# Cross output projection in token chunks, with part of the routing inside it, an earlier barrier, and SyncE's row stores ahead of two weight loads

## The chip, the cores and the metric

The kernel runs on one core of a Trainium2 chip. The metric is the device time of the whole program in microseconds. The program is one launch that runs both layers.

## The reference, cut to what matters

Two decoder layers run over 1024 prompt tokens and 32 sample tokens (1056 in all, model width 1024, float32). The end of each layer is this:

```python
x = x + cross_attn(rmsnorm(x, g_x), mem_k, mem_v, w_xq, w_xo)   # ends in o @ w_xo, 512 -> 1024
h = rmsnorm(x, g_ffn)
g_sel  = argmax(h @ w_rg + b_rg)                # 1 group of 4
e_logit = (h @ w_re + b_re) of the group g_sel  # 8 experts
top_p, top_i = top_k(softmax(e_logit), 2)       # 2 experts a token, gates from top_p
y = sum over both of gate * (silu(h @ w_eg[e]) * (h @ w_eu[e])) @ w_ed[e]
x = x + y
```

The 36 columns of w_rg and w_re together give the logits. 32 experts have 2 MB of gate and up weights and 1 MB of down weights each, so a layer reads 100 MB of them.

## The kernel before, in words

Every engine has its own program, and counters (semaphores) order them. Both layers run the same code.

**The projection.** `x` lies with the model width on the partitions: 8 blocks (`j`) by 1056 tokens. Blocks go one after the other. For each, TensorE computes three chunks of 352 tokens (`x_out`, L1392, 4 matmuls a chunk; a float32 matmul is two instructions in the trace) into one of two sets of three PSUM banks. VectorE adds all 1056 columns into `x` (L2522). ScalarE writes the block times its gain to `xn` (L1869) and its square to `xsq` (L1870). VectorE adds the squares to `xsum` (L2507, `add_xsq`). TensorE multiplies the router weights (36 columns, stationary) with `xn` (`logits`, L1403).

**Root and routing.** After the last block TensorE sums the squares by token (L1422), ScalarE takes the root (L1876), VectorE its reciprocal (L2530), and the logits are turned so that tokens lie on the partitions (L1427), nine tiles of 128 tokens, the last with 32. From L2533 to L2570 VectorE picks the group and the two experts of all nine tiles at once. TensorE counts picks by expert (L1445, L1447). VectorE ranks the experts by count (`place`, L2577 and L2578, 32 by 32 compares), works out a slot for each pick, and builds one-hot matrices that two TensorE matmul groups (L1457) turn into the table `idx` of token numbers (written at L2629).

**Rows to DRAM.** TensorE turns `xn` into token rows (`rows_of`, L1437), ScalarE scales them (L1886), and SyncE stores nine tiles to `xrow` (L684). Four row buffers are shared.

**The queue of SyncE**, in order: gate weights of experts 0 and 1 (L669, `load_gu`) after the first block; gate weights of experts 2 and 3 after the sums by token; nine row stores; down weights of experts 0 to 3 (L672, `load_dn`); when two gathers have landed (L689), gate weights of expert 4; when `routed` is set (L691), its down weights; then for each later expert, by popularity, a read of `order_i`, a wait for a free slot and its two loads. There are five slots. SyncE does nothing else while it waits, so everything behind a wait is held.

**The barrier.** When `idx` is ready, GpSimd starts the first two gathers of rows (L2874). VectorE goes on: the order of the experts (L2632 to L2635), the gates and the overflow list (L2637 to L2647, which sets `routed`), and only then `stage_end(dve, 9)`. All engines but SyncE wait there for each other. TensorE fills waits with idle matmuls (`keep_clock`, L777).

**The experts.** 22 blocks of 128 slots in each layer. For block n: TensorE turns the gathered rows (`turn_x`, L1470), VectorE copies them (`take_x`, L2654), TensorE does gate and up (L1484), ScalarE the exponential (L1896), VectorE `hidden` (L2660 to L2663), TensorE `turn_h` (L1494) and down (L1508), GpSimd scatters the result (L2880). Block n uses the experts of four groups: the first six experts have 3 or 4 groups each, the last nine 2 each. At the end of layer 0 SyncE also loads 5 MB for the next layer, whose first matmuls are L1547.

## Time and profile before

| what | value |
|---|---|
| median of 3 runs | 2490.47 us (2487.63 to 2491.78) |
| profiled execution, its own time | 2477.46 us |
| its span, first to last instruction | 2475.7 us |
| mean granted TensorE clock | 0.979 of full speed |
| TensorE busy | 2301.5 us, 93% |
| VectorE, ScalarE, GpSimd busy | 47%, 27%, 19% |
| stage of the change in layer 0 | about 824 to 940 us, experts to 1215 |
| same in layer 1 | about 2042 to 2157 us, experts to 2433 |

A timeline line is: start, duration, engine, line, operation, tiles, number of instructions, and in brackets the idle time before it and what ended it. A busy TensorE can be one that runs idle matmuls to keep its clock, so its share alone does not say what bounds a stage.

### The profile page before, as it was taken

The page shows a single profiled execution, that of the slowest core. Times are in us where ns is not written, and L with a number is a line of the kernel's source. Part 1 is how long each engine was busy: PE and PEld are TensorE (multiplying, and loading weights), DVE is VectorE, ACT ScalarE, POOL GpSimd, SP SyncE. Part 2 cuts the span into 40 slices and gives each one's busy share as a digit, 9 for nine tenths or more (in the row PEclk, how much of TensorE's full clock was granted, in tenths as well). Part 3 has the DMA queues.
Part 4 walks back from the last instruction along what each step waited for, and adds up shares of the span by engine and source line. Part 5 has one row for each costly group of instructions (what it writes and reads, how often), then busy time and mean ns, then how long its engine had stood idle before and what let it go on. Part 6 is the DMA issues. An engine that isn't in the chain of part 4 may idle for free.

```text
span 2475.7 us, 41476 instructions
## 1 busy us (share of the span) xinstructions
PE 2301.5 (93%) x17596; PEld 1359.3 (55%) x17596; DVE 1168.0 (47%) x2072; ACT 657.2 (27%) x1404; POOL 480.7 (19%) x590
## 2 busy tenths in 40 slices
PE   8999998889999999999899999988799999999984
PEld 5644565656666664333366456666566675733332
DVE  2455556874232354333263655568742342633334
ACT  1023554422012230111130335544220032211113
POOL 6003423520100001111260034235100000011113
PEclk9999999989999999999999999999899999999997
DMA  5001001163142148999840010011621411799996
GB/s 196 11 20 28 15 12 44 44 247 133 36 164 86 68 163 328 406 422 423 335 142 11 20 30 12 12 44 47 257 88 44 154 69 68 270 358 410 423 415 258
DMA packets 80288, 390.82 MB, mean 158 GB/s; under 512 B 20942, under 2 KB 25164, under 8 KB 60588
## 3 DMA queue, kind: packets, MB, share of 16 engines
q1 hardware_dynamic: 61948, 309.38, 32.5%
q0 software_dynamic: 17568, 76.57, 8.1%
q8 instruction: 143, 2.34, 0.4%
q10 hardware_dynamic: 576, 2.10, 0.2%
q14 instruction: 53, 0.43, 0.1%
HBM read 355.31 MB, written 41.41 MB: 160 GB/s over the span
## 4 chain that ended last, share of the span: by engine, by line
PE 76%; DVE 9%; issue 5%; ACT 3%; PEld 2%; DMA 2%; POOL 1%; POOLq 1%; PEldq 1%; SPq 0%; ACTq 0%; DVEq 0%
PE ps L1484 13%; PE ps L801 9%; PE ps L824 8%; PE ps L1508 6%; PE ps L1392 5%; PE ps L972 5%; PE ps L892 5%; PE ps L1192 3%; PE ps L984 2%; PE ps L950 2%; PE ps L1000 2%; PEld ps L824 2%; DVE arena L2225 2%; PE ps L1470 2%; PE ps L1214 1%
## 5 line engine op out<-in xcount | busy, mean ns | idle before, releaser
L1484 PE MATMUL ps<-arena 128*32 128x512 f32 x2304 | 316.9, 602 | 22.6 <-issue 16.8
L824 PE MATMUL ps<-arena,ring 128*128 128x352 f32 x936 | 277.9, 459 | 1.0 <-ACTq L489 1.0
L801 PE MATMUL ps<-x,ring 128*128 128x352 f32 x768 | 231.6, 463 | 11.1 <-DMA x<-in_x 9.6
L824 PEld LDWEIGHTS ps<-arena,ring 128*128 128x128 f32 x936 | 177.7, 190 | 99.4 <-ACTq L489 1.2
L2654 DVE COPY arena<-ps 128x1024 f32<-128x1024 f32 x44 | 53.9, 1224 | 336.9 <-PE ps L1470 336.9
L801 PEld LDWEIGHTS ps<-x,ring 128*128 128x128 f32 x768 | 146.9, 192 | 93.2 <-issue 13.3
L1484 PEld LDWEIGHTS ps<-arena 128*32 128x32 f32 x2304 | 92.4, 111 | 187.1 <-issue 187.1
L1508 PE MATMUL ps<-arena 128*32 128x512 f32 x1408 | 160.2, 595 | 3.8 <-ACT arena L1901 3.8
L2874 POOL DMA_INDIRECT arena<-xrow,arena x46 | 46.8, 1017 | 591.5 <-DVE arena L2629 319.9
L972 PE MATMUL ps<-arena 96*128 96x512 f32 (+3 forms) x384 | 144.9, 487 | 0.0
L1392 PE MATMUL ps<-arena,ring 128*128 128x352 f32 x384 | 117.7, 463 | 1.6 <-DVE arena L2487 1.6
L1484 PE MATMUL ps<-ring,arena 128*32 128x512 f32 x512 | 116.0, 607 | 0.0
L1670 ACT ACTIVATE ring<-ps 128x512 f32<-128x512 f32 (+2 forms) x192 | 87.7, 489 | 104.1 <-PE ps L984 104.1
L892 PE MATMUL ps<-arena,x 128*128 128x512 f32 x256 | 112.9, 601 | 2.2 <-ACT arena L1618 2.2
L1192 PE MATMUL ps<-arena 64*32 64x256 f32 x2560 | 90.2, 414 | 24.1 <-DVE arena L2359 15.1
L1675 ACT ACTIVATE ring<-ps,nmax 128x128 f32<-128x128 f32 (+7 forms) x128 | 94.7, 740 | 57.8 <-DVE nmax L2128 56.8
L2359 DVE STREAM_TRANSPOSE arena<-arena 128x1024 f32<-128x1024 f32 x80 | 95.9, 1227 | 24.4 <-PE ps L1192 23.1
L1896 ACT ACTIVATE arena<-ps 128x256 f32<-128x256 f32 x44 | 16.9, 383 | 329.1 <-PE ps L1484 329.1
L984 PE MATMUL ps<-consts,ring 128*128 128x128 f32 x576 | 89.7, 281 | 12.9 <-ACT ring L1670 6.5
L2127 DVE TENSOR_REDUCE nmax<-ps 128x1 f32<-128x128 f32 (+7 forms) x128 | 97.0, 758 | 4.4
L2126 DVE TENSOR_TENSOR ps<-ps,consts 128x128 f32<-128x128 f32 x128 | 38.2, 299 | 127.6 <-PE ps L972 126.5
L1392 PEld LDWEIGHTS ps<-arena,ring 128*128 128x128 f32 x384 | 71.7, 190 | 46.1 <-issue 6.8
(470 smaller groups left out, 3661.9 us busy)
## 6 DMA issues: line engine op xcount, KB each, us to landing
arena<-in_w_gu SPq DMA_DIRECT2D x52, 2048.0 KB, 14.3
arena<-in_w_dn SPq DMA_DIRECT2D x64, 1024.0 KB, 11.1
ring<-in_ring SPq DMA_DIRECT2D x56, 512.0 KB, 3.6
ring<-in_w_gu SPq DMA_DIRECT2D x12, 2048.0 KB, 13.9
arena<-yrow SPq DMA_DIRECT2D x16, 1024.0 KB, 9.3
arena<-in_mem_k SPq DMA_DIRECT2D x16, 512.0 KB, 7.2
arena<-in_mem_v SPq DMA_DIRECT2D x16, 512.0 KB, 9.2
xrow<-arena SPq DMA_DIRECT2D x16, 512.0 KB, 8.5
```

What stands on the lines that cost most here:

```text
L801: mm = pe.matmul(ps[:, PIECE_BANKS[n % len(PIECE_BANKS)], 0:CH], ring[:, j % RING, k, :], x[:, k, tok], start=k == 0, stop=k == KT - 1)
L824: mm = pe.matmul(ps[:, (j % 2) * NCH + c, 0:CH], ring[:, j // per, (j % per) * units + k, :], src[:, k, tok], start=k == k0, stop=k == uni ...
L892: mm = pe.matmul(ps[:, 6 + t % 2, :], x[:, k, t * P:t * P + m], wvg[:, k, :], start=k == 0, stop=k == KT - 1)
L972: mm = pe.matmul(ps[:, bank + at // 512, 0:end - at], q_h[0:QK, b, qb * P:(qb + 1) * P], k_h[0:QK, b, at:end], start=True, stop=True)
L984: mm = pe.transpose(ps[:, bank, (kb % 4) * P:(kb % 4 + 1) * P], prob[:, e, kb * P:(kb + 1) * P], ident)
L1192: mm = pe.matmul(ps[ND * g:ND * (g + 1), 4 + 2 * (n % 2) + h, 256 * x:256 * (x + 1)], q8[b][x][r, n, :], ct[r, m % NCT, 8 * g:8 * (g + 1), ...
L1392: mm = pe.matmul(ps[:, (j % 2) * NCH + c, 0:CH], ring[:, slot, (j % 2) * XH + k, :], co[:, k, tok], start=k == 0, stop=k == XH - 1)
L1484: mm = pe.matmul(ps[r, 2 + n % 2, :], xb_t[:, n % 2, k, r], w_gu[e % NW][:, k, :], start=k == 0, stop=k == KT - 1, skip_group_check=True)
L1508: mm = pe.matmul(ps[r, 4 + f, :], h_t[:, k, r], w_dn[e % NW][:, k, f * 512:(f + 1) * 512], start=k == 0, stop=k == 1, skip_group_check=True)
L1675: act.activation(prob[:, e, 0:w], ps[:, 2 * e:2 * e + 2, :].rearrange("p a n -> p (a n)")[:, 0:w], ACT.Exp, bias=nmax[:, e, 1:2], scale=ML ...
L2127: step(dve.reduce_max(nmax[:, e, 0:1], sc, AX))
L2359: dve.transpose(ct[:, m % NCT], keys).then_inc(ct_ready, 1)
```

## The change

The projection's loop is turned. Tokens are cut into tiles 0 to 2, 3 to 5 and 6 to 8 (384, 384 and 288 columns), and all eight blocks of one token chunk are done before the next: 24 units, three PSUM banks. Logits are computed with `xn` stationary and the router weights moving, so that they come out with tokens on the partitions. The turn of the logits and the copies before it go. After the fourth unit of the last chunk, root and routing of tiles 0 to 5 (`EARLY`) are done between the remaining units; tiles 6 to 8 follow after the last one. The counts and ranks are computed in two parts. `place` comes from a 32 by 32 compare with one column and a matmul. VectorE's barrier stands right after `idx`. The gates, the overflow list and `routed` move behind `hidden(0)`. In SyncE's queue the nine row stores come ahead of the gate weights of experts 2 and 3.

```diff
+XO_TILES = ((0, 3), (3, 6), (6, NT + 1))
+XO_UNITS = tuple((c, j) for c in range(len(XO_TILES)) for j in range(XO_MT))
+XO_BANKS = 3
+EARLY = XO_TILES[2][0]
...
-                sp.wait_ge(lin_done, IN_N + OUT_MT + XK_MT + XQ_MT + 1)
+                sp.wait_ge(xo_done, 1)
                 load_gu(0, 0)
                 load_gu(1, 1)
-                sp.wait_ge(ssq_ready, 2 * NCH + 1)
-                load_gu(2, 2)
-                load_gu(3, 3)
                 for t in range(NT + 1):
                     m = P if t < NT else ND
                     sp.wait_ge(xr_evac, t + 1)
                     sp.dma_start(xrow[t * P:t * P + m, :], xr[0:m, t % 4, :]).then_inc(row_moved[t % 4], 16)
+                load_gu(2, 2)
+                load_gu(3, 3)
                 for e in range(4):
                     load_dn(e, e)
...
+                def logits(u):
+                    c, k = XO_UNITS[u]
+                    pe.wait_ge(xg_ready, u + 1)
+                    for t in range(*XO_TILES[c]):
+                        m = P if t < NT else ND
+                        mm = pe.matmul(ps[0:m, 3 if t < EARLY else 4, t * NR:(t + 1) * NR], xn[:, k, t * P:t * P + m], w_r[:, k, :],
+                                       start=k == 0 and t in (0, EARLY), stop=k == KT - 1, skip_group_check=True)
...
+                for u in range(len(XO_UNITS)):
+                    x_out(u)
+                    if u == 0:
+                        x_back(NT)
+                    if u >= 1:
+                        logits(u - 1)
+                    if XO_UNITS[u] == (2, 2):
+                        pe.wait_ge(sq_added, NCH + 1 + 2)
+                        token_sums(0, EARLY)
+                keep_clock(3, 4)
+                pe.wait_ge(sq_added, NCH + 1 + 3)
+                token_sums(EARLY, NT + 1)
+                logits(len(XO_UNITS) - 1)
...
-                for t in range(6):
+                for t in range(5):
                     rows_of(t)
-                keep_clock(5, 9)
                 pe.wait_ge(part_or_counts_ready, len(PART) + 1)
+                count_tiles(0, EARLY, 0)
+                rows_of(5)
+                pe.wait_ge(part_or_counts_ready, len(PART) + 2)
+                count_tiles(EARLY, NT + 1, 1).then_inc(ranked, 1)
+                count_above(0, EARLY)
+                count_above(EARLY, NT + 1).then_inc(ranked, 1)
-                keep_clock(3, 12)
+                keep_clock(3, 3)
+                pe.wait_ge(beaten_or_hot_ready, 1)
+                pe.matmul(ps[:, 2, 0:NE], ones[0:NE, :], beaten[0:NE, :], start=True, stop=True).then_inc(ranked, 1)
...
-                keep_clock(3, 34)
+                keep_clock(3, 22)
                 stage_end(pe, 9)
...
+                for u in range(len(XO_UNITS)):
+                    add_out(u)
+                    if u >= 1:
+                        add_xsq(u - 1)
+                    if XO_UNITS[u] == (2, 3):
+                        dve.wait_ge(std_ready, 2 * NCH + 1)
+                        step(dve.reciprocal(rstd_t[:, 0:EARLY], rstd_t[:, 0:EARLY]))
+                        dve.sem_inc(norm_ready, 1)
+                        dve.wait_ge(lg_done, 1)
+                        take_logits(0, EARLY, 3)
+                    elif XO_UNITS[u] == (2, 4):
+                        pick_group(0, EARLY)
+                    elif XO_UNITS[u] == (2, 5):
+                        first_of_max(e_all, NE, 0, EARLY, m1, oh1)
+                    elif XO_UNITS[u] == (2, 6):
+                        pick_second(0, EARLY)
+                        step(count_picks(0, EARLY))
...
-                step(dve.tensor_tensor(beats, key.unsqueeze(1).broadcast_to([P, NE, NE]), key.unsqueeze(2).broadcast_to([P, NE, NE]), ALU.is_gt))
-                step(dve.tensor_reduce(place, beats, AX, ALU.add))
+                step(dve.tensor_tensor(key_own[0:NE, :], key[0:NE, :], ident[0:NE, 0:NE], ALU.mult))
+                step(dve.tensor_reduce(key_col[0:NE, :], key_own[0:NE, :], AX, ALU.add))
+                dve.tensor_scalar(beaten[0:NE, :], key[0:NE, :], key_col[0:NE, 0:1], None, ALU.is_lt).then_inc(beaten_or_hot_ready, 1)
+                dve.wait_ge(ranked, 3)
...
                 dve.tensor_copy(idx, table).then_inc(idx_ready, 1)
 
+                stage_end(dve, 9)
+
...
-                dve.tensor_copy(over_i[:, :], over_c).then_inc(routed, 1)
-                step.restart()
-                stage_end(dve, 9)
-
+
+                def weigh_and_spill():
+
+                    dve.wait_ge(rx_out, 1)
...
+                    dve.tensor_copy(over_i[:, :], over_c).then_inc(routed, 1)
...
                     hidden(n)
+                    if n == 0:
+                        weigh_and_spill()
```

## Rows read from the trace of the kernel before

**Rows 1.** The page's first line.

```profile
span 2475.7 us, 41476 instructions
```

**Rows 2.** Windows: stretch, length, five engines' busy time, clock, DMA share, GB/s.

```profile
955.00:960.00 5.00, 5.00 (x50) 2.20 (x42) 0.00 (x0) 0.73 (x2) 0.00 (x0) 1.00 0.46 175
960.00:990.00 30.00, 30.00 (x277) 10.27 (x280) 12.08 (x15) 4.51 (x7) 6.07 (x6) 1.00 0.94 362
990.00:1150.00 160.00, 160.00 (x1456) 56.24 (x1452) 55.33 (x68) 23.42 (x41) 27.40 (x27) 1.00 1.01 416
...
2180.00:2210.00 30.00, 30.00 (x280) 10.21 (x276) 10.00 (x13) 4.51 (x7) 5.09 (x5) 1.00 0.95 369
```

**Rows 3.** Timeline of TensorE where the experts of layer 0 end.

```profile
1164.65 8.77 PE L1484 MATMUL ps<-arena 128*32 128x512 f32 x64 [2.47 <-issue]
...
1217.78 13.99 PE L1547 MATMUL ps<-arena 128*128 128x512 f32 x32 [3.23 <-issue]
```

**Rows 4.** Timelines of VectorE, GpSimd and TensorE around the barrier of layer 0.

```profile
932.05 0.21 DVE L2629 CAST arena<-arena 128x92 int32<-128x92 f32 x1
...
939.38 0.18 DVE L2647 CAST over_i<-arena 128x25 int32<-128x25 f32 x1
...
954.07 0.42 DVE L2663 TENSOR_TENSOR arena<-ps,arena 128x256 f32<-128x256 f32 x1
...
933.16 1.21 POOL L2874 DMA_INDIRECT arena<-xrow,arena  x1 [159.69 <-DVE arena L2629]
...
939.66 1.09 PE L1470 MATMUL ps<-consts,arena 128*128 128x128 f32 x8 [0.92 <-DVEq L489]
942.23 7.07 PE L1484 MATMUL ps<-arena 128*32 128x512 f32 x64 [1.48 <-DVE arena L2654]
```

**Rows 5.** Timeline of SyncE's DMA queue in layer 0.

```profile
833.26 67.32 SPq L669 DMA_DIRECT2D arena<-in_w_gu  x4
901.89 20.26 SPq L684 DMA_DIRECT2D xrow<-arena  x9
922.19 3.07 SPq L672 DMA_DIRECT2D arena<-in_w_dn  x4
938.95 0.33 SPq L669 DMA_DIRECT2D ring<-in_w_gu  x1
...
949.52 9.82 SPq L669 DMA_DIRECT2D arena<-in_w_gu  x2
```

**Rows 6.** Gathers (L2874) issued at 934.67, at 951.10, and 17 from 984 to 1175.

```profile
DMA to landing us min/median/max: 4.2/4.2/4.2
...
DMA to landing us min/median/max: 8.5/8.5/8.5
...
DMA to landing us min/median/max: 9.3/10.6/12.2
```

**Rows 7.** Timeline of TensorE in the projection and the sums by token, layer 0.

```profile
875.92 7.37 PE L1392 MATMUL ps<-arena,ring 128*128 128x352 f32 x24
883.22 1.37 PE L1403 MATMUL ps<-arena 128*36 128x352 f32 x6
...
893.13 1.38 PE L777 MATMUL ps<-consts 128*128 128x128 f32 x10
...
896.86 2.10 PE L1422 MATMUL ps<-consts,arena 128*128 128x1 f32 x18
```

**Rows 8.** Timelines of ScalarE and VectorE in the routing of layer 0.

```profile
896.78 1.28 ACT L1876 ACT_TABLE_LOAD   x1
...
899.24 0.21 DVE L2530 RECIPROCAL arena<-arena 128x9 f32<-128x9 f32 x1 [2.09 <-ACT arena L1877]
...
904.97 0.46 DVE L2550 TENSOR_TENSOR arena<-arena 128x288 f32<-128x288 f32 x1
...
909.20 0.46 DVE L2570 TENSOR_TENSOR arena<-arena 128x288 f32<-128x288 f32 x1
...
912.18 1.23 DVE L2577 TENSOR_TENSOR arena<-arena 128x1024 f32<-128x1024 f32 x1
```

More of the change, by code:

```diff
@@ L1388, in x_out @@
                     if j == 0:
-                        last = max(i for i, t in enumerate(X_ORDER) if t * P < tok.stop and t * P + P > tok.start)
-                        pe.wait_ge(xot_evac, last + 1)
+                        pe.wait_ge(xot_evac, max(X_ORDER.index(t) for t in range(*XO_TILES[c])) + 1)
+                    if u >= XO_BANKS:
+                        pe.wait_ge(xo_added, u - XO_BANKS + 1)
                     for k in range(XH):
-                        mm = pe.matmul(ps[:, (j % 2) * NCH + c, 0:CH], ring[:, slot, (j % 2) * XH + k, :], co[:, k, tok],
+                        mm = pe.matmul(ps[:, u % XO_BANKS, 0:tok.stop - tok.start], ring[:, slot, (j % 2) * XH + k, :], co[:, k, tok],
@@ new lines, in token_sums, with count_tiles @@
+                def token_sums(first, end):
+                    for t in range(first, end):
+                        m = P if t < NT else ND
+                        mm = pe.matmul(ps[0:m, 5, t:t + 1], xsum[:, t * P:t * P + m], ones[:, 0:1], start=True, stop=True)
+                    mm.then_inc(ssq_ready, 1)
+                def count_tiles(first, end, by_tile):
+                    for a, z, m in ((first, min(end, NT), P), (NT, end, ND)):
+                        if z <= a:
+                            continue
+                        counted = pe.matmul(ps[:, 5, 0:NE * (NT + 2)].rearrange("p (e t) -> p e t", e=NE)[:, :, a + by_tile:z + 1], ones[0:m, :],
+                                            both[0:m, a + by_tile:z + 1, :].rearrange("p t e -> p e t"), start=True, stop=True)
+                    return counted
@@ new lines, in count_above @@
+                def count_above(first, end):
+                    for a, z, m in ((first, min(end, NT), P), (NT, end, ND)):
+                        if z <= a:
+                            continue
+                        counted = pe.matmul(ps[:, 4, a * NE:z * NE], con("below", m), both[0:m, a + 1:z + 1, :].rearrange("p t e -> p (t e)"),
+                                            start=True, stop=True)
+                    return counted
+                for u in range(len(XO_UNITS)):
+                    x_out(u)
+                    if u == 0:
+                        x_back(NT)
[4 more added lines that the diff above has]
+                        token_sums(0, EARLY)
@@ L2569, in _ @@
-                step.sync()
-                dve.tensor_tensor(both[:, 1:NT + 2, :], oh1, oh2, ALU.add).then_inc(part_or_counts_ready, 1)
+                dve.wait_ge(std_ready, 2 * NCH + 3)
+                dve.reciprocal(rstd_t[:, EARLY:NT + 1], rstd_t[:, EARLY:NT + 1]).then_inc(norm_ready, 1)
+                dve.wait_ge(lg_done, 2)
+                dve.wait_ge(norm_ready, 2 * NCH + 2)
+                take_logits(EARLY, NT + 1, 4)
+                pick_group(EARLY, NT + 1)
+                first_of_max(e_all, NE, EARLY, NT + 1, m1, oh1)
@@ L2597, in _ @@
                                        cum[:, :, 0:NT + 1].rearrange("p e t -> p t e"), ALU.add))
[L2598 to L2600 removed]
+                step.mark(dve.tensor_tensor(rank, above, every(base, 0, NT + 1), ALU.add))
+                step(dve.tensor_tensor(r_tmp, above, every(cap, 0, NT + 1), ALU.is_ge))
+                step(dve.tensor_tensor(r_tmp, r_tmp, every(jump, 0, NT + 1), ALU.mult))
                 step(dve.tensor_tensor(rank, rank, r_tmp, ALU.add))
```

217 lines of the change are left out of this document (102 added, 115 removed).

## The prediction, made before the changed kernel was run

> **What bounds the kernel now.** I read the windows first, then the timelines of all engines around the barrier, then the landings of transfers. The trace's span is 2475.7 us [rows 1] and its own time 2477.5 us, 0.5% under the median of the runs shown (2490.5). I work against 2477.5 and carry the difference over to the median.
>
> The stage behind the barrier is the important one. From 990 to 1150 us the DMA engines' share is 1.01 at 416 GB/s while TensorE is also busy all the time [rows 2]. Both look full, and the end of the stage says which one is the limit: there TensorE sits idle until weights come, with no engine named as the releaser, once for 2.47 us and, before the next layer's matmuls, for 3.23 us [rows 3]. So TensorE lives on loads made early, and the transfers are always behind. Nothing done sooner on TensorE moves that end; what moves it is time in which the DMA engines have nothing to do near the start. They have some: the share is 0.46 from 955 to 960 and 0.94 from 960 to 990 [rows 2]. Layer 1 shows the same (0.95 from 2180 to 2210).
>
> Ahead of that, `idx` is written at 932.26 us, the gathers start at 933.16, VectorE reaches its barrier after 939.38, and `turn_x(0)` begins at 939.66 [rows 4]. The second gather landed 4.2 us after its issue at 934.67 [rows 6], at 938.9, and SyncE issued expert 4's gate weights at 938.95 [rows 5]. So the early barrier can at best save from 939.66 down to where the first gather lands.
>
> **The projection and routing: nothing gained.** 24 matmul instructions on 352 columns take 7.30 us from start to start [rows 7], 0.304 each. Scaled by columns, 128 of 384 and 64 of 288 columns are 42.5 + 15.9 = 58.4 us, as before (8 x 7.30). The logits become 24 units x 3 tiles x 2 = 144 instructions with 128 stationary columns. The nearest row is the sum by token, which also loads 128 columns for a narrow product: 2.10 us for 18, 0.117 each [rows 7]. That is 16.8 us against 8 x 1.37 = 11.0 before. Below 0.117 lies only the time of 36 moving columns (36/352 of 0.304, 0.03), which would need the weight loads to vanish; I take 0.117. Early sums add 12 x 0.117 = 1.4 and 18 idle matmuls leave, 18 x 0.138 = 2.5. With the last unit's logits behind the sums, TensorE is through with its units at 896.9 + 16.1 + 1.4 - 11.0 - 2.5 = 901 us.
>
> VectorE is later still. Its nine-tile routing took from 899.45 to 909.66, 10.2 us [rows 8]. A step costs about 0.21 at 9 elements and 0.46 at 288, so 0.38 at 192 and 0.29 at 96. Six tiles take about 8 us, three about 6 (the four clears of padding go too). The early 8 us, the wait for ScalarE's root (some 2.4 us, 1.28 of it the load of its function table [rows 8]), and the last four units' adds of residual and squares, 8 x 0.46 = 3.7, all stand on VectorE from about 889.5 on. They end near 903.5, so the late sums come at about 903.8 instead of 896.9, and the late reciprocal at 905 instead of 899.24. Then 6 us instead of 10.2: the counts are asked for at 911 against 909.7. `rows_of(5)` stands ahead of them on TensorE and costs up to another 1. `place` saves: two steps of 1.23 [rows 8] become three of 0.2 and a tiny matmul with its two handovers, 1.1 to 1.4 less. The sum is +1.3 + 0.8 - 1.3 = +0.8. TensorE is some 2 us earlier at its 72 idle instructions ahead of the one-hot matmuls, because it no longer waits for row stores, and that gives back about 0.5. `idx` comes at 932.5, that is where it was; I keep -1.5 and +2 for the range. TensorE idles about 3 us ahead of the late sums. A gap of 2.47 us left 64 instructions at 8.77 us instead of 7.07 [rows 3, 4]. Such a 1.7 us, most of it beside VectorE's chain, is inside the +2.
>
> **SyncE's queue.** Before, gate weights 2 and 3 (4.2 MB) went out before the rows, in the hole of the sums, and the down weights from 922.19 [rows 5]. They were nearly through when the gathers came. Now all 8.4 MB follow the ninth row store, which can leave at about 919.5. ScalarE's rows no longer wait for the stores behind 4 MB of weights, which frees 2.6 us, but rows are not on the way to `idx`. 8.4 MB at 416 GB/s [rows 2] is 20 us: the DMA engines are full until about 941, and the gathers are issued at 933.4 into that. The rows for such a gather: 8.5 us beside one gate load, 9.3 to 12.2 in the full stage [rows 6]. I take 8.5, because the backlog ends soon; below lies 4.2, above 10.6. So `xb` is there at about 941.8 and `turn_x(0)` starts then, 2.1 us later than now, though the barrier opens 7 us sooner.
>
> The Trainium skill (DMA: Bandwidth & Descriptors, Queues, rings and completion order) says that each DMA engine alternates between the queues that have work. By that rule alone, with an even split, the 0.5 MB gather would need 2 x 1.3 us of transfer and land after about 4 to 5 us, which is the second rival below. The 8.5 and 9.3 us rows speak against an even split here.
>
> **The move of `routed`: the loss.** SyncE waits for `routed` before expert 4's down weights, and every later load is behind that in its queue. Before it was set at 939.56, and expert 5's gate weights left at 949.52 as soon as block 0 had freed the slot [rows 5]. Now `routed` follows `hidden(0)`. `hidden(0)` ends at 954.49, which is 14.8 us after `turn_x(0)` began; the moved work is 3.4 us, that is 939.56 less 932.26 less the order of the experts, three steps of 1.23 and one of 0.2 [rows 4, 8], which stays where it was. So `routed` comes 18.2 us after `turn_x(0)`: at 960.0. At that point 3.15 MB are unsent that the kernel before had already sent: 7.5 us of transfers. What the old kernel leaves idle after that is open to catch up in: 0.06 x 30 = 1.8 us until 990 [rows 2], then nothing. TensorE does not stall at once, since expert 5 is first needed by block 3. The debt is paid at the end of the stage. So a layer ends 7.5 - 1.8 = 5.7 us later. With the catch-up uncertain by half a microsecond I take 5.5. Both layers have the same queue and shares, so 2 x 5.5 = +11: 2488.5 for the profiled execution and 2501 for the median.
>
> **Rivals.**
> *The debt stays and the gather is quick* (4.2 us). Then `turn_x(0)` starts at 937.3 and `routed` comes at 955.5. The idle time that can be used grows by 0.54 x 4.5 = 2.4 (955 to 960), and what the old kernel still had in flight at 955.5 is about 1.5. The layer loses 7.5 - 1.5 - 1.8 - 2.4 = 1.8: +3.6 us, 2494, 0.14%, no difference that can be told. The row of 4.2 speaks for it, the 8.4 MB at the same time against.
> *TensorE, not the transfers, paces the experts.* Then the debt costs nothing and the early barrier shows: with a quick gather `turn_x(0)` goes from 939.66 to 937.3, 2 x 2.4 = 4.8 us, 2485.5, just faster. This needs both a DMA share under 1 in the middle of the stage and waits that do not grow at its end. The share of 1.01 speaks against it [rows 2].
> *The early routing takes the routing off the path.* If VectorE were not late behind the last unit, the late chain would be 4.2 us shorter, `idx` at 928, `turn_x(0)` at 933 with a quick gather. `routed` at 951.3 then leaves a gain of about 2.5 us a layer, 2485.5. It decides the sign only if `turn_x(0)` comes before about 935.8. My order of VectorE's work speaks against it.
> *More than one cost at once:* a gather of 10.6 us and `idx` 1.5 us late start `turn_x(0)` at 945 and `routed` at 963.6; with 1.6 us to catch up in, and 3.6 us more debt, 9.3 us a layer, 2509.
>
> **Chances and range.** The forecast, a debt of 4 to 7 us a layer, 0.56. The late case 0.10. The quick gather 0.18, of which a third would still be past 0.2% as slower (0.05) and 0.13 within. The two rivals that end faster have 0.09 and 0.05. 0.02 is left for gains and debts that cancel. 0.2% is 5 us, about what a measurement of this kernel can tell from no change. So slower 0.56 + 0.10 + 0.05 = 0.71, same 0.13 + 0.02 = 0.15, faster 0.14. For 8 in 10 the range reaches from the middle of the quick gather and its neighbours, 2487, to the late case, 2508. The likeliest case's own range is 2497 to 2505.
>
> **What would show it.** Right: `idx` within 2 us of 932; a gather of 8 us or more; `routed` about 18 us after `turn_x(0)`; a hole in SyncE's queue between expert 4's gate weights and its down weights with a low DMA share; expert 5's gate weights near 960; more idle time of TensorE in the last blocks. Wrong: a gather of 4 us, a DMA share well under 1 from 990 on, or `idx` before 929. If the stage's end moves by much less than the hole, the transfers were not the limit there.

## The result and the profile after

The changed kernel takes 2518.61 us, median of four runs (2517.10 to 2520.14), against 2489.55 (2487.63 to 2491.78) for the kernel before beside it. The ratio is 1.012 with a 95% interval of 1.0106 to 1.0134: slower by 29 us. I had forecast slower by 11. The profiled execution took 2520.14 us.

The page's first line:

```profile
span 2517.9 us, 41790 instructions
```

**Where the time went.** I cut each layer at its own marks and counted from the start of the projection, because the profiled executions differ ahead of it: it begins at 824.4 us in the trace before and at 828.95 after. Layer 0 / layer 1, in us, worked out from the start times of the instructions (the last row is the start of the last instruction of the last down block; it ends 0.6 later):

| from the projection's start to | before | after | forecast |
|---|---|---|---|
| `idx` | 107.6 / 108.1 | 109.4 / 110.8 | 108.0 |
| `turn_x(0)` | 115.3 / 115.9 | 122.1 / 123.2 | 117.4 |
| `routed` | 115.0 / 115.6 | 145.6 / 146.7 | 135.6 |
| the last down block | 389.6 / 390.5 | 406.2 / 407.5 | 395.1 |

The stage grew by 16.6 + 17.0 = 33.6 us. The spans differ by 42.2; the other 8.6 lie outside. Two profiles of the kernel before differ by 5.8 us there (the control run at the end), so I don't put the 8.6 down to the change. Marks come from one execution each: the stage grew by 33.6 us in them, the medians by 29, and in the experiments below the marks show between 0 and 7 us more than the ratio of the times.

The queue of SyncE and the landing of the two gathers, to be held against [rows 5, 6]:

```profile
912.51 13.43 SPq L686 DMA_DIRECT2D xrow<-arena  x9
925.99 0.94 SPq L674 DMA_DIRECT2D arena<-in_w_gu  x2
926.97 2.41 SPq L677 DMA_DIRECT2D arena<-in_w_dn  x4
950.98 0.33 SPq L674 DMA_DIRECT2D ring<-in_w_gu  x1
974.73 0.33 SPq L677 DMA_DIRECT2D arena<-in_w_dn  x1
976.12 1.48 SPq L674 DMA_DIRECT2D arena<-in_w_gu  x2
```

```profile
DMA to landing us min/median/max: 10.1/10.1/10.1
```

The six loads (8.4 MB) leave behind the ninth row store. Between expert 4's gate weights at 950.98 and its down weights at 974.73 nothing leaves for 23.7 us. Before it was 0.63 us (938.95 to 939.58). The timelines of the other engines around the barrier answer to [rows 4]:

```profile
938.31 0.21 DVE L2706 CAST arena<-arena 128x92 int32<-128x92 f32 x1
951.06 1.23 DVE L2711 TENSOR_TENSOR arena<-ps,arena 128x1024 f32<-128x1024 f32 x1 [12.54 <-POOLq L494]
...
955.05 1.22 DVE L2733 COPY arena<-ps 128x1024 f32<-128x1024 f32 x1
...
970.97 0.42 DVE L2742 TENSOR_TENSOR arena<-ps,arena 128x256 f32<-128x256 f32 x1
...
974.52 0.18 DVE L2729 CAST over_i<-arena 128x25 int32<-128x25 f32 x1
...
940.83 0.99 POOL L2955 DMA_INDIRECT arena<-xrow,arena  x1 [0.30 <-issue]
...
951.08 1.97 PE L1494 MATMUL ps<-consts,arena 128*128 128x128 f32 x8 [8.65 <-POOLq L494]
956.42 9.78 PE L1508 MATMUL ps<-arena 128*32 128x512 f32 x64 [3.37 <-DVE arena L2733]
```

VectorE is at its barrier at 938.5 and then sits for 12.54 us, TensorE for 8.65. Both were released by GpSimd's sequencer (POOLq, L494 is the barrier's helper). GpSimd issues both gathers, then drains, then arrives, and its arrival comes when the gathers have landed: 940.83 + 10.1 = 950.9. The chain of waits has one piece there:

```profile
940.52 10.52 POOLq L494
```

So the new barrier on VectorE opened nothing sooner. Behind it the three long ordering steps and the copy of the order, 951.06 to 955.02, stand ahead of the evacuation of `turn_x(0)` at 955.05. And TensorE comes back slow. The windows (stretch, length, five engines' busy time, granted clock, DMA share, GB/s), to be held against [rows 2]:

```profile
940.00:945.00 5.00, 2.44 (x22) 2.25 (x21) 0.00 (x0) 0.00 (x0) 1.51 (x2) 0.99 1.02 427
945.00:950.00 5.00, 0.00 (x0) 0.00 (x0) 0.00 (x0) 0.00 (x0) 0.00 (x0) 0.50 0.90 367
950.00:955.00 5.00, 1.97 (x8) 1.57 (x8) 3.83 (x4) 0.00 (x0) 0.99 (x1) 0.50 0.63 224
955.00:960.00 5.00, 3.58 (x20) 1.12 (x24) 1.24 (x2) 0.00 (x0) 0.00 (x0) 0.50 0.60 248
960.00:965.00 5.00, 5.00 (x44) 1.46 (x39) 0.00 (x0) 0.00 (x0) 0.00 (x0) 0.81 0.00 0
965.00:970.00 5.00, 3.59 (x36) 1.57 (x32) 2.70 (x3) 0.38 (x1) 0.99 (x1) 1.00 0.09 16
...
990.00:1150.00 160.00, 160.00 (x1462) 55.67 (x1455) 55.03 (x69) 23.73 (x40) 27.83 (x28) 1.00 1.01 422
```

TensorE goes idle at 942.4. Windows of 1 us show the granted clock at 0.93 from 944 to 945, then at 0.50 (1.2 of 2.4 GHz) until about 962, 17 us in all. TensorE is busy again from 956.42 on; `gate_up(0)` takes 9.78 us instead of 7.07. The DMA engines, full at 1.02 until 945, carry next to nothing from 960 on, until the down weights leave at 974.73. From 990 to 1150 they are full and TensorE is busy all the time, as before: nothing is caught up there. The rest of the bill comes where the experts end. Three waits stand there, the first as in [rows 3]; these are all three of the changed kernel, and the second one of the kernel before:

```profile
1185.46 9.61 PE L1508 MATMUL ps<-arena 128*32 128x512 f32 x64 [6.38 <-issue]
...
1201.13 0.62 PE L1508 MATMUL ps<-arena 128*32 128x512 f32 x2 [1.25 <-issue]
...
1217.10 8.77 PE L1508 MATMUL ps<-arena 128*32 128x512 f32 x64 [4.08 <-issue]
```

```profile
1181.58 0.66 PE L1484 MATMUL ps<-arena 128*32 128x512 f32 x2 [3.35 <-issue]
```

Waits of 2.47, 3.35 and 2.38 us, 8.2 in all, have become 6.38, 1.25 and 4.08, 11.7 in all. That is not the whole 16.6. The rest is already there when `turn_x(1)` starts, in the trace before and in the one after:

```profile
949.23 1.09 PE L1470 MATMUL ps<-consts,arena 128*128 128x128 f32 x8
```

```profile
966.13 1.09 PE L1494 MATMUL ps<-consts,arena 128*128 128x128 f32 x8
```

From the projection's start these are 124.8 and 137.2 us. From here to `turn_x(19)` both traces take 208.3 us, 11.7 a block, with one idle time of 1.4 us. So TensorE's late start, 12.4 us, is handed on undiminished, and 4.2 come at the end, 3.5 of them as waits.

The transfers tell the same lateness. Add up GB/s by length over windows from 75 to 175 us after the projection's start: 27.4 and 27.2 MB against 33.8 and 33.9 before. The missing 6.4 and 6.7 MB are 15 and 16 us at 422 GB/s, and the last down block came 16.6 and 17.0 later.

### The profile page after: what moved, and what is told of

Same layout as the page of the kernel before. It is cut to its first block, busy times and chain, and to the rows that moved or that the text cites. A ratio compares the mean times of both kernels' runs of the same rounds, so it can differ in the third digit from the quotient of the medians.

```text
span 2517.9 us, 41790 instructions
## 1 busy us (share of the span) xinstructions
PE 2318.8 (92%) x17650; PEld 1378.2 (55%) x17650; DVE 1177.5 (47%) x2192; ACT 667.1 (26%) x1464; POOL 480.3 (19%) x590
## 4 chain that ended last, share of the span: by engine, by line
PE 73%; DVE 11%; issue 5%; ACT 3%; PEld 2%; POOLq 2%; DMA 1%; POOL 1%; PEldq 1%; SPq 0%; ACTq 0%; DVEq 0%
PE ps L1508 13%; PE ps L804 9%; PE ps L827 8%; PE ps L1532 6%; PE ps L975 5%; PE ps L895 4%; PE ps L1395 4%; PE ps L1195 4%; PE ps L987 2%; PE ps L953 2%; PE ps L1003 2%; PEld ps L827 2%; DVE arena L2267 2%; POOLq L494 2%; PE ps L1494 1%
## 5 line engine op out<-in xcount | busy, mean ns | idle before, releaser
L1508 PE MATMUL ps<-arena 128*32 128x512 f32 x2304 | 324.1, 619 | 32.9 <-issue 23.4
L827 PE MATMUL ps<-arena,ring 128*128 128x352 f32 x936 | 277.9, 459 | 1.0 <-ACTq L494 1.0
L804 PE MATMUL ps<-x,ring 128*128 128x352 f32 x768 | 231.8, 463 | 12.3 <-DMA x<-in_x 10.9
L827 PEld LDWEIGHTS ps<-arena,ring 128*128 128x128 f32 x936 | 177.7, 190 | 99.4 <-ACTq L494 1.2
L804 PEld LDWEIGHTS ps<-x,ring 128*128 128x128 f32 x768 | 147.0, 192 | 94.6 <-issue 14.8
L1532 PE MATMUL ps<-arena 128*32 128x512 f32 x1408 | 160.2, 595 | 3.8 <-ACT arena L1943 3.8
L1395 PE MATMUL ps<-arena,ring 128*128 128x384 f32 (+1 forms) x384 | 125.3, 469 | 0.0
L1195 PE MATMUL ps<-arena 64*32 64x256 f32 x2560 | 99.6, 409 | 20.0 <-DVE arena L2401 14.7
L1949 ACT ACTIVATE arena<-ps 128x1024 f32<-128x1024 f32 x44 | 45.0, 1024 | 179.5 <-PE ps L1532 179.5
```

The source lines that it names most:

```text
L804: mm = pe.matmul(ps[:, PIECE_BANKS[n % len(PIECE_BANKS)], 0:CH], ring[:, j % RING, k, :], x[:, k, tok], start=k == 0, stop=k == KT - 1)
L827: mm = pe.matmul(ps[:, (j % 2) * NCH + c, 0:CH], ring[:, j // per, (j % per) * units + k, :], src[:, k, tok], start=k == k0, stop=k == uni ...
L1195: mm = pe.matmul(ps[ND * g:ND * (g + 1), 4 + 2 * (n % 2) + h, 256 * x:256 * (x + 1)], q8[b][x][r, n, :], ct[r, m % NCT, 8 * g:8 * (g + 1), ...
L1395: mm = pe.matmul(ps[:, u % XO_BANKS, 0:tok.stop - tok.start], ring[:, slot, (j % 2) * XH + k, :], co[:, k, tok], start=k == 0, stop=k == X ...
L1508: mm = pe.matmul(ps[r, 2 + n % 2, :], xb_t[:, n % 2, k, r], w_gu[e % NW][:, k, :], start=k == 0, stop=k == KT - 1, skip_group_check=True)
L1532: mm = pe.matmul(ps[r, 4 + f, :], h_t[:, k, r], w_dn[e % NW][:, k, f * 512:(f + 1) * 512], start=k == 0, stop=k == 1, skip_group_check=True)
```

## The experiments

Eleven kernels that undo or do one part, and a control. All times, the ratios to runs of the kernel before on the same chip, and the marks of layer 0 / 1 in us from the projection's start (MB: moved from 75 to 175 us after it). The kernel before had medians of 2483 to 2485 us beside the experiments, 4 to 6 less than beside the changed kernel, so ratios are compared and not times; a ratio is not exactly the quotient of the two medians.

| run | median us | ratio, 95% interval | `idx` | `turn_x(0)` | `routed` | last down | MB |
|---|---|---|---|---|---|---|---|
| changed | 2518.61 | 1.012, 1.0106 to 1.0134 | 109 / 111 | 122 / 123 | 146 / 147 | 406.2 / 407.5 | 27.4 / 27.2 |
| e1 | 2512.70 | 1.0102, 1.0066 to 1.0138 | 111 / 109 | 124 / 122 | 144 / 143 | 404.2 / 403.7 | 28.0 / 28.9 |
| e2 | 2512.95 | 1.0109, 1.0081 to 1.0138 | 116 / 115 | 123 / 122 | 146 / 145 | 406.6 / 406.4 | 27.2 / 27.8 |
| e3 | 2514.42 | 1.0118, 1.0086 to 1.0149 | 109 / 109 | 122 / 122 | 129 / 129 | 406.3 / 405.7 | 28.1 / 28.3 |
| e4 | 2501.24 | 1.0077, 1.0050 to 1.0104 | 111 / 109 | 123 / 122 | 118 / 117 | 401.5 / 398.5 | 29.7 / 30.7 |
| e5 | 2498.28 | 1.0058, 1.0038 to 1.0078 | 107 / 107 | 121 / 120 | 114 / 115 | 401.3 / 396.5 | 30.2 / 31.4 |
| e6 | 2504.78 | 1.0063, 1.0039 to 1.0087 | 116 / 114 | 123 / 122 | 123 / 122 | 400.1 / 398.3 | 29.8 / 30.7 |
| e7 | 2496.38 | 1.0041, 1.0026 to 1.0056 | 107 / 107 | 115 / 115 | 137 / 138 | 399.1 / 398.3 | 31.1 / 31.1 |
| e8 | 2509.17 | 1.0087, 1.0065 to 1.0109 | 116 / 116 | 125 / 126 | 134 / 135 | 403.5 / 403.6 | 28.9 / 29.1 |
| e9b | 2490.94 | 1.0030, 1.0016 to 1.0044 | 107 / 107 | 115 / 115 | 115 / 115 | 395.3 / 394.6 | 31.8 / 32.1 |
| e10b | 2482.60 | 0.9995, 0.9980 to 1.0009 | 107 / 107 | 114 / 115 | 122 / 124 | 389.6 / 389.3 | 34.7 / 34.2 |
| e11b | 2487.50 | 1.0020, 1.0005 to 1.0034 | 111 / 109 | 116 / 115 | 124 / 123 | 393.8 / 394.5 | 32.6 / 33.4 |
| e12b | 2482.81 | 0.9996, 0.9980 to 1.0011 | 109 / 107 | 117 / 115 | 117 / 115 | 391.2 / 389.0 | 33.2 / 34.6 |

**e1, the gathers behind the barrier (changed kernel).**

```diff
                 pool.wait_ge(idx_ready, 1)
+                stage_end(pool, 9)
                 for n in range(2):
                     gather(n)
-                stage_end(pool, 9)
```

> The changed kernel, but GpSimd passes the barrier before it starts the first two gathers. Barrier theory (the barrier opens only when GpSimd's drain has seen its two gathers land, and VectorE's ordering of the experts then stands ahead of take_x(0)): the barrier opens within 1 us of idx, VectorE's four ordering steps (3.9 us) run beside the gathers, and turn_x(0) starts with the first gather instead of the second. That gives 3 to 6 us a layer, 2507 to 2513. Queue theory (the gathers are late only because of the weight loads ahead of them, the barrier costs nothing): GpSimd's gathers start 0.3 us later, 2518 to 2520.

```profile
951.97 1.94 PE L1494 MATMUL ps<-consts,arena 128*128 128x128 f32 x8 [9.05 <-DMA arena<-xrow,arena]
955.39 8.64 PE L1508 MATMUL ps<-arena 128*32 128x512 f32 x64 [1.48 <-DVE arena L2733]
```

Now the barrier opens when TensorE's 44 idle instructions end, at 943, the gathers leave at 943.76 and 945.16, and `turn_x(0)` waits for the gather itself (a DMA as the releaser). It comes no sooner. The first load left at 926.48, and the gathers land 25.4 and 25.9 us after it; in the changed kernel, issued 4 us sooner, they land 24.9 us after it. The wait is the backlog, whoever holds it. What was gained, 1.9 us of order steps that no longer stand ahead of the evacuation and 1.1 of clock, shows as `routed` 20.5 us behind `turn_x(0)` in place of 23.4. The last down block comes 2.0 and 3.8 us sooner; the ratio, 1.0102, can't be told from 1.012.

**e2, SyncE's old order (changed kernel).**

```diff
+                sp.wait_ge(ssq_ready, 2 * NCH + 2)
+                load_gu(2, 2)
+                load_gu(3, 3)
                 for t in range(NT + 1):
...
-                load_gu(2, 2)
-                load_gu(3, 3)
```

> The changed kernel, with SyncE's old order: gate weights of experts 2 and 3 after the late sums by token, then the row stores. Queue theory: the DMA engines are through before the gathers start, these land in 4 to 5 us instead of 10, turn_x(0) starts some 6 us sooner, TensorE's clock does not fall before block 0, and routed comes 7 to 9 us sooner: 2501 to 2505. Theory of the moved routed (the hole in SyncE's queue is the whole loss and it is as long wherever turn_x(0) stands): 2516 to 2519.

```profile
922.50 4.74 PE L1459 MATMUL ps<-consts,arena 128*128 128x128 f32 x24 [5.72 <-ACT arena L1929]
```

The gathers land after 4.3 us, as forecast. But the row stores stand behind 4.2 MB again, ScalarE's rows wait for them, and in this kernel TensorE's instructions for rows stand among the counts: it idles 5.72 us and `idx` comes 4 to 7 us later. One cost replaces the other, and the 2501 to 2505 us that I expected were missed. My working had it that rows are not on the way to `idx`; behind the chunked projection with the old queue they are.

**e3 and e4, `routed` ahead of the experts again.** e3 puts the gates and the overflow flag between the ordering and `take_x(0)`, behind VectorE's early barrier. e4 also moves this barrier back behind them.

```diff
+                weigh_and_spill()
...
-                    if n == 0:
-                        weigh_and_spill()
```

> The changed kernel, with the gates, the overflow list and routed after the order of the experts and ahead of take_x(0), still behind the barrier. Debt theory (what waits for routed in SyncE's queue is repaid at the end of the stage): block 0 starts 3.4 us later, but expert 4's down weights leave 16 us sooner and expert 5's gate weights right after block 0's gate and up, so the DMA engines are idle for some 7 us less: 5 to 7 us a layer, 2505 to 2509. If TensorE's start sets the end of the stage instead: 3.4 us a layer later, 2525.

> The changed kernel, with VectorE's old tail: order, gates, overflow list and routed all ahead of its barrier. Barrier theory: the gathers hold the barrier 12 us anyway, so the 7.3 us of VectorE's work fit into that wait, the barrier opens at the same time, take_x(0) comes 3.8 us sooner and routed 28 us sooner: 9 to 12 us a layer, 2495 to 2500, the rest being the slow gathers. If the early barrier is worth what it was worth on paper (7 us a layer) and only the queue is at fault: 2520 or more.

Timelines of SyncE and TensorE in e3:

```profile
954.66 0.33 SPq L677 DMA_DIRECT2D arena<-in_w_dn  x1
965.96 9.81 SPq L674 DMA_DIRECT2D arena<-in_w_gu  x2
...
955.90 9.82 PE L1508 MATMUL ps<-arena 128*32 128x512 f32 x64 [6.67 <-DVE arena L2735]
```

e3 teaches most. `routed` is 16 us sooner than in the changed kernel and nothing is gained. With all of the tail behind the late barrier, block 0 starts 8.6 us behind `turn_x(0)`, and expert 5's gate weights need the slot that block 0's 64 matmuls free: they leave at 965.96. The stream needs two releases, `routed` and the end of the first `gate_up`. Helping one by delaying the other leaves the same hole. TensorE is late too: `turn_x(1)` starts at 140.5, 3.3 us later than in the changed kernel. In e4 VectorE does the tail while GpSimd waits for its gathers anyway, and 0.43 of the 1.2% come back, by the ratios. In the stage that is 4.7 and 9.0 us, less than the 9 to 12 a layer that I expected.

**e5, SyncE's new order alone, in the kernel before.**

```diff
-                sp.wait_ge(ssq_ready, 2 * NCH + 1)
-                load_gu(2, 2)
-                load_gu(3, 3)
                 for t in range(NT + 1):
...
+                load_gu(2, 2)
+                load_gu(3, 3)
```

> The kernel before, with SyncE's new order alone: nine row stores, then the gate weights of experts 2 and 3, then the down weights. Queue theory: 8.4 MB stand in the DMA queue from the ninth row store on, so both gathers land when that backlog is through, at about 118 us after the projection's start instead of 114.5; VectorE's tail hides in the wait; TensorE idles 3 us more and block 0 runs partly at the lower clock: 3 to 5 us a layer, a ratio of 1.0025 to 1.004. If the order costs nothing by itself: 1.000.

```profile
930.52 1.21 POOL L2873 DMA_INDIRECT arena<-xrow,arena  x1 [159.32 <-DVE arena L2628]
...
943.15 1.97 PE L1469 MATMUL ps<-consts,arena 128*128 128x128 f32 x8 [7.05 <-POOLq L489]
946.60 9.98 PE L1483 MATMUL ps<-arena 128*32 128x512 f32 x64 [1.48 <-DVE arena L2653]
```

Half of the loss with nothing else of the change: 0.58%, more than the 0.25 to 0.4% that I expected. The gathers are issued at 930.52 and 932.03 and land at 943.0, 26.3 us after the first load (916.65), and the same two things follow, TensorE's idle time and the slow `gate_up(0)`.

**e6, the chunked projection alone** (e2's edit and e4's together).

> The changed kernel with the old tail and the old order of SyncE: what is left is the chunked projection with the early routing. From the second experiment: rows 4 to 8 wait for stores that stand behind 4 MB of weights, the idle matmuls and one-hot matmuls stand behind these rows on TensorE, and idx comes 8 us late; the gathers land in 4 us; order and gates are ahead of the barrier: 8 us a layer, ratio 1.006 to 1.007. If the projection alone is neutral, as I predicted (0.3 us a layer): 1.000.

The ratio of 1.0063 is as expected. The kernel inherits e2's late rows, `idx` at 114 to 116, so it doesn't price the projection by itself; e11b does that better.

**e7, the early barrier and late `routed` alone, in the kernel before.** The overflow list is also built elsewhere in its buffer, which the cut below leaves out, as it does the old place of the moved steps.

```diff
                 dve.tensor_copy(idx, table).then_inc(idx_ready, 1)
+                stage_end(dve, 9)
...
                     hidden(n)
+                    if n == 0:
+                        weigh_and_spill()
```

> The kernel before, with VectorE's barrier right after idx and the gates, the overflow list and routed behind hidden(0); nothing else (the overflow list is built 828 words further on in the buffer). Debt theory: turn_x(0) starts 0.5 us sooner, take_x(0) 2 us later behind the order of the experts, routed 22 us later, so expert 4's down weights and expert 5's gate weights leave 12 to 20 us later: 7 to 9 us a layer, ratio 1.006 to 1.007. If the early barrier is a gain and routed was never waited for: 0.998.

```profile
940.85 0.33 SPq L669 DMA_DIRECT2D ring<-in_w_gu  x1
963.32 0.33 SPq L672 DMA_DIRECT2D arena<-in_w_dn  x1
...
940.96 1.09 PE L1470 MATMUL ps<-consts,arena 128*128 128x128 f32 x8 [0.55 <-POOLq L489]
946.29 8.50 PE L1484 MATMUL ps<-arena 128*32 128x512 f32 x64 [4.25 <-DVE arena L2656]
```

With a quick gather (4.9 us) the barrier opens when it lands, no sooner than before. The gap in the queue is 22.5 us, and it costs 0.41%, 10 us, less than the 0.6 to 0.7% expected, though the marks show the expected 7.8 and 9.5 us a layer. Not all of it is the hole: the ordering steps make TensorE wait 4.25 us ahead of `gate_up(0)`, and `turn_x(1)` starts 3.5 us late. e5 and e7 together are 0.99% of the 1.2%.

**e8, a mended tail with SyncE's old order** (changed kernel: e1's and e2's edits, three of the four ordering steps, the gates and the flag between `take_x(0)` and `take_x(1)`).

> The changed kernel with three edits: SyncE's old order, GpSimd's gathers behind its barrier, and VectorE's tail cut in two: the first ordering step ahead of take_x(0), the other three and gates, overflow list and routed between take_x(0) and take_x(1), where VectorE has 7 us to spare. Debt theory: routed comes 8 us after turn_x(0) instead of 23.5, so the debt is gone; idx still comes 8 us late for the row stores: 7 to 9 us a layer over the kernel before, ratio 1.006 to 1.007, that is 11 us less than the changed kernel. If only TensorE's start counts: 1.009.

A miss: 1.0087 (1.0065 to 1.0109), where 1.006 to 1.007 was expected. `idx` was late as in e2, and TensorE's idle instructions ahead of its barrier, unmoved, now held the barrier.

**e9b, the hole by itself.** One wait in the kernel before; the programs of TensorE and VectorE stay as they were.

```diff
                 sp.wait_ge(routed, 1)
+                sp.wait_ge(gu_done, 2)
                 load_dn(4, 4)
```

> The kernel before, with one wait on SyncE: the down weights of expert 4, and with them every later weight load, leave only when expert 1's gate and up products are done, so 3.15 MB of down weights and what follows leave some 10 to 20 us later than they do before. Nothing else is changed. If a hole in the weight stream is what costs (debt theory), the wait costs some 7.5 us of transfers in each layer less 2.1 us of idle time there already, 5.4 us a layer, and the ratio is 1.004 to 1.0045, with TensorE's early blocks where they were and the last experts late. If the time is set by when block 0 starts, the ratio is 1.000.

```profile
950.00:955.00 5.00, 3.59 (x33) 1.51 (x29) 2.62 (x3) 0.39 (x1) 0.99 (x1) 1.00 0.09 13
955.00:960.00 5.00, 5.00 (x52) 1.89 (x48) 1.40 (x3) 0.00 (x0) 0.00 (x0) 1.00 0.19 63
```

```profile
960.88 0.33 SPq L672 DMA_DIRECT2D arena<-in_w_dn  x1
...
939.94 1.10 PE L1471 MATMUL ps<-consts,arena 128*128 128x128 f32 x8 [0.97 <-POOLq L489]
942.51 8.77 PE L1485 MATMUL ps<-arena 128*32 128x512 f32 x64 [1.48 <-DVE arena L2655]
```

`turn_x(0)` and `gate_up(0)` start where they did. `gate_up(0)` takes 8.77 us instead of 7.07, because the granted clock is 0.50 from 943 to 946 here, which it was not in the trace before with nearly the same idle times ahead of it (0.97 and 1.48 us here, 0.92 and 1.48 there); `turn_x(1)` still starts at 126.1 and 126.0, within the 124.6 to 126.5 of the two profiles of the kernel before. The down weights leave at 960.9, almost where I had forecast `routed` for the changed kernel (960.0). The last down block comes at 395.3 and 394.6 instead of 389.0 to 391.2 (kernel before, two profiles): 5 us a layer, where the debt gives 5.4. The ratio is 1.003, its interval holds the first theory's lower end and leaves 1.000 out. TensorE was busy from 955 to 990 all the same. So idle time of the transfers alone, beside a TensorE that is no later than it can be in the kernel before, makes the stage longer.

**e10b, the tail split, in the kernel before.** The mend of e7 (its buffer move is in here too, and the removal of the steps from their old place is again left out of the cut):

```diff
-                keep_clock(3, 34)
                 stage_end(pe, 9)
+                keep_clock(3, 26)
...
                 dve.tensor_copy(idx, table).then_inc(idx_ready, 1)
+                stage_end(dve, 9)
...
                 take_x(0)
+                step(dve.tensor_tensor(beats, beats, iota[:, 0:NE].unsqueeze(1).broadcast_to([P, NE, NE]), ALU.mult))
+                step(dve.tensor_reduce(order_f, beats, AX, ALU.add))
+                step(dve.tensor_copy(order_i[:, :], order_f))
+                weigh_and_spill()
                 for n in range(NB):
...
+                stage_end(pool, 9)
                 for n in range(2):
                     gather(n)
-                stage_end(pool, 9)
```

> The kernel before with the barrier passed right after the row indices by VectorE and GpSimd, the gathers behind it, 26 idle matmuls behind TensorE's barrier in place of the 34 ahead of it, one ordering step ahead of the first row transpose, and the other ordering steps, the gates, the overflow test and the copy of its flag between the first and the second row transpose. SyncE's queue is that of the kernel before. If what costs in the changed tail is the hold of the barrier by the gathers and the late flag, this is not slower: 0.998 to 0.9995. If splitting the routing costs by itself, 1.002 or more.

```profile
932.71 6.07 PE L777 MATMUL ps<-consts 128*128 128x128 f32 x52 [1.42 <-POOLq L489]
...
941.13 7.07 PE L1484 MATMUL ps<-arena 128*32 128x512 f32 x64 [1.48 <-DVE arena L2653]
```

`turn_x(0)` starts at 938.62. The barrier does open early here, at 932.7, and TensorE's idle matmuls run through the gather's landing, so the clock stays at full speed. `routed` comes 8.2 us behind `turn_x(0)`, ahead of the slot's release at 948. It holds expert 4's down weights for 7.4 us, most of which the gate weights ahead of them fill (a DMA share of 0.89 and 0.71 from 940 to 950), and no later load. 0.9995 (0.998 to 1.0009): the whole cost of e7 is gone, and there is no gain that can be told. The 34.7 and 34.2 MB moved are those of the kernel before (33.2 to 34.6 in two profiles).

**e11b, the changed kernel mended.** e1's and e10b's edits, and this queue for SyncE behind its nine row stores:

```diff
                 load_gu(2, 2)
-                load_gu(3, 3)
-                for e in range(4):
+                for e in range(2):
                     load_dn(e, e)
                 for p in range(2):
                     sp.wait_ge(xb_full[p], 16)
+                load_gu(3, 3)
+                load_dn(2, 2)
                 load_gu(4, 4)
+                load_dn(3, 3)
```

> The changed kernel with its chunked projection and its nine row stores first, but with the gathers behind the barrier, the idle matmuls behind TensorE's barrier, the ordering steps split about the first row transpose, and SyncE's queue in this order: nine row stores, gate weights of expert 2, down weights of experts 0 and 1; then, when the two gathers have landed, gate weights of 3, down weights of 2, gate weights of 4, down weights of 3; then, when the overflow flag is there, down weights of 4. If the queue order and the barrier make up the whole of the cost, the ratio is 0.998 to 1.002. If the chunked projection has a cost of its own, 1.004 or more.

```profile
930.00:935.00 5.00, 3.20 (x32) 2.82 (x32) 2.99 (x7) 0.00 (x0) 1.10 (x1) 1.00 0.42 172
935.00:940.00 5.00, 3.97 (x36) 3.72 (x34) 0.92 (x1) 0.00 (x0) 1.25 (x2) 1.00 0.47 140
```

```profile
940.45 7.07 PE L1510 MATMUL ps<-arena 128*32 128x512 f32 x64 [1.48 <-DVE arena L2732]
```

1.002 (1.0005 to 1.0034): of the 1.2%, 0.2 remain. The gathers land after 4.4 us, and TensorE keeps full clock from 910 to 955. What remains is a share of 0.42 and 0.47 while the weights wait for the gathers, and `idx` 1 to 3 us later than in the kernel before. No version is faster than the kernel before by more than the noise.

**e12b, the control:** the kernel before, run as an experiment.

> The kernel before, unchanged, as a control: from the output projection to the last down block 389 to 391 us in both layers, and outside this stretch up to 6 us a layer between profiles of one kernel. The ratio is 1.000.

0.9996 (0.998 to 1.0011). The stretch from the projection to the last down block is 391.2 and 389.0 (389.6 and 390.5 in the trace before); `idx` came at 109.3 in one layer and 107.2 in the other. From the first matmuls behind the experts (L1547) to the next layer's attention scores (L1314) it took 777.0 us against 772.1 in the trace before: that is most of the 5.8 us by which the two profiles differ outside the stage.

## Why the prediction was wrong in size

**What held.** A hole near the start of the stage is paid at its end. From 175 to 350 us after the projection's start the DMA share is 0.98 or more in every run, so bytes that have not moved by then stay late: the megabytes missing, at 422 GB/s, match the lateness within 3.5 us a layer in every run. e9b shows the hole alone, at 4 to 6 us a layer. The projection's working held too, counted from its start: TensorE through with its units at 76.2 (forecast 76.6); the late sums at 79.6 (79.4); the late reciprocal at 80.6 (80.6); the counts asked for at 87.1 (86.6). These are its rows, against [rows 7, 8]:

```profile
836.15 2.83 PE L1395 MATMUL ps<-arena,ring 128*128 128x384 f32 x8
838.82 0.75 PE L1407 MATMUL ps<-arena 128*128 128x36 f32 x6
839.40 2.83 PE L1395 MATMUL ps<-arena,ring 128*128 128x384 f32 x8
...
908.53 0.76 PE L1416 MATMUL ps<-consts,arena 128*128 128x1 f32 x6 [2.24 <-DVE arena L2560]
909.58 0.18 DVE L2638 RECIPROCAL arena<-arena 128x3 f32<-128x3 f32 x1 [0.75 <-ACT arena L1917]
```

From start to start, eight instructions on 384 columns take 2.67 us, 0.334 each (0.332 forecast), and six logits 0.58, 0.097 each (0.117 forecast). `idx` came at 109.4 and 110.8 against 108.0, 1.4 and 2.8 later, where I had kept 2 in the range. In layer 0 VectorE waits 2.94 us for the counts from TensorE, where it waited 1.42 before: row transposes stand ahead of them, and from 911 to 913 they run at a granted clock of 0.50.

**The step that failed** is the time of `routed`, 135.6 forecast and 145.6 measured in layer 0. Its three terms:

1. `idx`, 1.4 later.
2. "`xb` is there at about 941.8 and `turn_x(0)` starts then, 2.1 us later than now, though the barrier opens 7 us sooner." From `idx` to `turn_x(0)` I had 9.3 us, it took 12.8: 3.5 more. I priced the gather by one row, 8.5 us, "because the backlog ends soon". I had the ninth store leaving at 919.5, which is 95.1 from the projection's start. It left just ahead of 97.0, and 8.4 MB behind it take 20 us. A gather issued into it lands when the backlog does: 24.9, 25.9 and 26.3 us after the first load in the changed kernel, e1 and e5, though the second of the pair was issued 14.8, 18.7 and 15.4 us after it. Rows for a gather beside one load don't price one behind six. And the barrier did not open sooner: GpSimd arrives at it behind both gathers and a drain. In the trace before this was hidden, since its gathers landed at 938.9 and VectorE came last, at 939.56. I moved one engine's arrival and didn't ask who comes second.
3. "`routed` comes 18.2 us after `turn_x(0)`." It came 23.4 after. The part that I moved took 3.4 us, as forecast (971.31 to 974.70), but `hidden(0)` ended 20.3 behind `turn_x(0)` and not 14.8. Of these 5.5 us, 2.8 are the ordering steps. I wrote that they "stayed where they were"; in the code they did, but with the barrier opening late they stood between it and the evacuation of `turn_x(0)`, where before they were done under the gather. The other 2.7 are the clock, 9.78 us for `gate_up(0)` against 7.07.

The sum is 1.4 + 3.5 + 5.2, 10 us in layer 0 (`routed` is 11.1 late in layer 1). The debt per us of hole was about right: from e9b to the changed kernel the down weights leave 10.0 us later in layer 0, and the last down block comes 10.9 later. So my 5.5 became 15 to 16, which is what the megabytes say. Twice the missing 10 us is 20; with the 11 forecast, 31, and 29 was measured.

**A term that I put at nothing.** I wrote that nothing done sooner on TensorE moves the end, and gave a later start no price. The forecast start of 2.1 us later fits into the 8.2 us of waits at the end. The measured one, 12.4 us at `turn_x(1)`, does not: from the traces I estimate that by itself, with every load on time, it would have cost at least 4 us a layer. No run delays TensorE and leaves the transfers alone, so how the 16.6 us would part is not shown. In these kernels both are late together, since the slot for expert 5's weights comes free only when `gate_up(0)` is done.

**The rivals.** The quick gather is real where nothing is queued: 4.3 us in e2, 4.4 in e11b. With the new queue it was never to be had. The late case (gather 10.6, `routed` at 963.6, 2509) was the right mechanism; it left out the barrier, the ordering steps and the clock (and its own terms, 7.5 + 3.6 - 1.6, give 9.5 us a layer and not 9.3). That TensorE alone paces the experts is ruled out for the kernel before by e9b; in the changed kernel the waits at the end have grown too, 11.7 us from 8.2, so the transfers still end last there.

**The round robin.** I set the rule of the Trainium skill (DMA: Bandwidth & Descriptors, Queues, rings and completion order) aside with a sum in bytes. The packets of the changed kernel by queue, from 944 to 946 us:

```profile
q1 hardware_dynamic: 83, 0.60, 71.4%
q0 software_dynamic: 86, 0.23, 29.6%
```

q1 carries the weights, q0 the gathers. Turns are even, 83 packets to 86, and bytes are not, 0.60 MB to 0.23. The Trainium skill says there that turns go by packet. If the packets that the profile counts are the same thing, which no run shows, rule and trace agree in counts; I had read "an even split" of bytes into it. The pair of gathers is 288 packets and 0.70 MB (I had taken 0.5 MB for one gather). Alone in the trace before, 175 of them pass in the 2 us from 936 to 938; beside the weights, 86. So a shared gather runs at half its own speed, 6 to 7 us instead of 3.3, and it started late as well: of the 288 packets only 12 had moved by 944, 3.2 us after the second issue. What these first 3 us are was not tested.

**Open.** The chunked projection was never timed without its neighbours. `idx` stands at 109.3 to 110.8 in the runs with it and the new queue, and at 107.2 to 109.3 without it. e4 against e5 (0.77 and 0.58%) and e11b, which holds a hole of its own (0.2%), put it at about 5 us in all or less. By the intervals it could be nothing or some 8 us. One part of it can be seen: ahead of the late sums TensorE idles 2.24 us in the changed kernel, and in it and in e11b the granted clock is down to 0.50 for 3 to 7 us there, in both layers. In two profiles of the kernel before, four layers, it is down for 3 to 4 us in two of them.

## What to carry to other kernels

Before an engine's barrier is moved ahead, list what each of the other engines does between its last real work and its arrival: an arrival behind a drain waits for the DMAs issued ahead of it, and the second-latest engine sets what can be gained. Before a load queue is shifted, look at what small latency-bound transfer is issued into it: it pays for the backlog ahead of it, not for its own size. And where transfers bound a stage, find every semaphore that the load queue waits for near the stage's start; the time in which the transfers run dry there comes back at the end, less what idle time later on lets them catch up, even if the compute engines never stall beside it. Then compare a late start of the compute engine with its waits at the stage's end: they hide the start only up to their own length.

## What the runs showed of the hardware

- A pair of gathers (288 packets, 0.70 MB) landed in 4.1 to 4.9 us on free DMA engines (kernel before, e2, e7, e9b, e10b, e11b) and in 8.4 to 10.9 issued at the same point with 8.4 MB ahead of it (changed kernel, e3, e5). From 944 to 946 us of the changed kernel the two queues moved 86 and 83 packets, of 2.7 and 7.2 KB.
- GpSimd's arrival at the barrier, a drain behind two indirect gathers, came when these had landed, 9.2 us after the second issue had ended; moved ahead of the gathers (e1), it no longer held the barrier.
- TensorE's granted clock fell to 0.50 about 2.5 us into an idle time of 8.65 us and stayed there for some 17 us; it rose again 5.5 us after `gate_up(0)` had started. 64 matmuls on 512 columns took 9.78 us instead of 7.07; in e10b, with idle matmuls through the same stretch, 7.07.
- Logits with the tokens stationary and 36 columns moving cost 0.097 us per instruction beside 384-column matmuls, from start to start.
